# Where the end of a sliding-window attention stage puts its low parts, its last value banks and its first logits

## The reference, cut to what matters

```python
q, k, v, z = split(x @ w_in, [1024, 1152, 1280])        # 16 query heads, 2 key heads of 64; z is 1024 wide
q, k = rope(q), rope(k)
s = einsum(q_block, k_block_and_previous) * 64 ** -0.5   # window 128, blocks of 128 tokens
s = where(0 <= i + 128 - j < 128, s, -inf)
p = softmax(concat([s, sink]))[..., :-1]
o = einsum(p, v)
y = (o * silu(z)) @ w_out                                # 1024 x 1024
x = layernorm(4 ** 0.25 * x + y) * g + b
```

## Time and profile before

| what | before |
|---|---|
| three executions | 1002.01 to 1003.83 us, median 1003.71 |
| the profiled execution | 1004.43 us, of which its span 1002.7 us |
| busy of the span | PE 97%, DVE 64%, ACT 45%, POOL 34% |
| mean granted TensorE clock | 0.993 |
| matmuls, busy in 900 to 920 us | 12.01 of 20 us, clock 0.83 |
| matmuls, busy in 920 to 980 us | 60.00 of 60 us, clock 1.00 |

### The profile page before, as it was taken

The page is one execution under the profiler, slowest core; times in us unless marked ns, Lnnn a source line. Parts: engine busy times, 40 slices in busy tenths (PEclk is TensorE's granted clock), DMA queues, the critical chain, the costliest instruction groups (busy, mean ns, idle before and its releaser), DMA issues.

```text
span 1002.7 us, 19936 instructions
## 1 busy us (share of the span) xinstructions
PE 967.8 (97%) x7678; PEld 797.3 (80%) x7678; DVE 646.7 (64%) x1197; ACT 450.5 (45%) x1301; POOL 337.4 (34%) x642
## 2 busy tenths in 40 slices
PE   7999999999999999999999999999999999996997
PEld 6888788787878787888888888888787777775885
DVE  4677858686766777664457656653435678778755
ACT  5656456565667565655356211321214555564000
POOL 1008484846565555646100000100012353546000
PEclk9999999999999999999999999999999999998999
DMA  6233412314142314141303412320305010123111
GB/s 215 65 82 92 104 60 63 102 39 126 33 111 54 110 36 130 30 114 42 96 22 100 153 42 64 85 53 1 95 22 106 24 44 24 49 75 113 63 42 63
DMA packets 95181, 73.80 MB, mean 74 GB/s; under 512 B 32848, under 2 KB 84208, under 8 KB 95088
## 3 DMA queue, kind: packets, MB, share of 16 engines
q1 hardware_dynamic: 60768, 55.69, 19.1%
q10 hardware_dynamic: 34320, 16.84, 6.6%
HBM read 61.47 MB, written 11.04 MB: 72 GB/s over the span
## 4 chain that ended last, share of the span: by engine, by line
PE 81%; DVE 8%; ACT 6%; DMA 3%; issue 2%; ACTq 0%; DVEq 0%
PE ps L805 28%; PE ps L992 15%; PE ps L1165 9%; PE ps L1064 9%; PE ps L1005 2%; PE ps L1187 2%; PE ps L1149 2%; DVE tok L1577 2%; PE ps L962 1%; DMA ws_raw<-in_b_w_in 1%; PE ps L973 1%; PE ps L971 1%; PE ps L882 1%; PE ps L950 1%; PE ps L949 1%
## 5 line engine op out<-in xcount | busy, mean ns | idle before, releaser
L805 PE MATMUL ps<-act_hi,w_hi 128*128 128x512 f32 x512 | 224.2, 438 | 0.4 <-DVE w_lo L1528 0.4
L805 PE MATMUL ps<-act_hi,w_lo 128*128 128x512 f32 x512 | 201.6, 394 | 0.0
L805 PE MATMUL ps<-act_lo,w_hi 128*128 128x512 f32 x512 | 200.5, 392 | 0.0
L707 POOL TENSOR_TENSOR rank<-inverse,tok 128x60 f32<-128x60 f32 (+24 forms) x248 | 95.5, 385 | 97.9 <-DMA tok<-blocks_in 79.6
L1577 DVE SCALAR_TENSOR_TENSOR tok<-xs,convw,tok 128x512 f32<-128x512 f32 x144 | 116.3, 808 | 15.7 <-ACT xs L1290 13.7
L805 PEld LDWEIGHTS ps<-act_hi,w_lo 128*128 128x128 f32 x512 | 96.4, 188 | 21.4
L710 POOL TENSOR_TENSOR inverse<-inverse,rank 128x60 f32<-128x60 f32 (+24 forms) x248 | 102.0, 411 | 19.4
L805 PEld LDWEIGHTS ps<-act_hi,w_hi 128*128 128x128 f32 x512 | 97.3, 190 | 12.4 <-issue 0.6
L805 PEld LDWEIGHTS ps<-act_lo,w_hi 128*128 128x128 f32 x512 | 97.5, 190 | 10.0
L992 PE MATMUL ps<-wo_hi,act_hi 128*128 128x512 f32 x224 | 89.1, 398 | 8.9 <-DVE act_lo L1669 7.0
L992 PE MATMUL ps<-wo_lo,act_hi 128*128 128x512 f32 x224 | 88.2, 394 | 1.0 <-ACT bT L1490 1.0
(11 more groups left out here) (265 smaller groups left out, 2115.0 us busy)
## 6 DMA issues: line engine op xcount, KB each, us to landing
w_raw<-in_a_w_in ACTq DMA_DIRECT2D x32, 512.0 KB, 4.2
tok<-in_x SPq DMA_DIRECT2D x8, 512.0 KB, 7.4
decay<-gc_rows SPq DMA_DIRECT2D x8, 512.0 KB, 5.4
tok<-blocks_in SPq DMA_DIRECT2D x32, 128.0 KB, 2.7
v_turn<-v_tok SPq DMA_DIRECT2D x8, 512.0 KB, 6.4
v_tok<-v_turn SPq DMA_DIRECT2D x32, 128.0 KB, 3.0
xres<-in_x SPq DMA_DIRECT2D x8, 512.0 KB, 3.6
ws_raw<-in_b_w_in SPq DMA_DIRECT2D x16, 256.0 KB, 2.7
```

The source lines that it names most:

```text
L707: inner.next(pool.tensor_tensor(part, inverse[:, 0:rows, m:m + 1].broadcast_to([P, rows, w]), blocks[:, m:m + 1, m + 1:32].broadcast_to([P ...
L805: mm = pe.matmul(ps[:, g % 2, :], lhs[:, k, :], rhs[:, k, HALF * b:HALF * (b + 1)], start=(i == 0), stop=(i == GROUP - 1))
```

## The change

It has five parts.

1. `low_wo` of slices 1 to 7 goes from GpSimd to VectorE, among `low_out` and `apply_gate`: slices 1 and 2 by hand, slices 3 to 7 in `out_stage`, with one of the last three `apply_gate` behind each of slices 3, 4 and 5. The low part of slice 0 moves ahead of the last logits' second unit. `w_out` is fetched through two buffers and no longer three.
2. After `out_pair(1, 2)` TensorE makes slices 0, 1 and 2 of token tile 2; from slice 3 on it makes three token tiles per slice, and tiles 3 to 7 follow one by one.
3. `last_rows_bank` of pair 14 is bank 4, and that of pair 15 stays so; the first `out_step` no longer waits for `s_e` and `s_ob3`. For this the sides of all units are swapped (`unit`, `place`), and `values(14)` waits for all exponentials.
4. `logits(0)` is made after the projection of token tile 20, three projections ahead of the last. The mask of unit 0 and its maximum come ahead of the last rope on VectorE, its exponentials ahead of the last transpose's copy on ScalarE, where a small Exp after tile 20 precedes them. `TURN_BANKS` uses bank 5 in place of 3 from tile 16 on.
5. The 7 low parts of the gate weights go from GpSimd to VectorE, behind the first `inverted` of each even pair.

The core of the diff (in the new code `logits`, `exponentials` and `biased` only stand earlier in the file):

```diff
-TURN_BANKS = [2 + n % 2 for n in range(3 * NT - 3)] + [5, 5, 6]
+TURN_BANKS = [(2, 3 if n < 2 * NT else 5)[n % 2] for n in range(3 * NT - 3)] + [5, 5, 6]
+EARLY_LOGITS = 20
-EARLY, EARLY_OUT = (3, 2), (3, 3)
-OUT_SLOT = ((0, 1, 2, 0, 1, 0, 1, 3), (0, 1, 2, 0, 1, 2, 0, 1))
+EARLY, EARLY_OUT = (3, 3), (3, 3)
+OUT_SLOT = ((0, 1, 2, 0, 1, 0, 1, 3), (0, 1, 0, 1, 0, 1, 0, 1))
 def unit(v):
-    return k, (k + v) % 2, k // NT, k % NT
+    return k, (k + v + 1) % 2, k // NT, k % NT
 def last_rows_bank(k):
-    return 4 if k == PAIRS - 1 else 1 + 2 * ((k + 1) % 2)
+    return 4 if k >= PAIRS - 2 else 1 + 2 * (k % 2)
...
@@ gpsimd, the loop over units
-                if v % 4 == 0 and v // 4 + 1 < NK:
-                    low_gate(v // 4 + 1)
-            for k in range(1, NK):
...
-                pool.tensor_tensor(wo[1][1][k][:, :], out_raw[1][OUT_SLOT[1][k]], wo[1][0][k][:, :].bitcast(F32),
-                                   ALU.subtract).then_inc(L[1]["wolo"], 1)
@@ tensor, out_stage
                 for k in range(2 * i, NK):
                     out_pair(i, k)
-                for t in range(2, NT):
+                    if i == 1:
+                        if k == 2:
+                            pe.wait_ge(s_ob, PAIRS)
+                            pe.wait_ge(s_ob3, PAIRS)
+                            out_step(1, 2, 0)
+                            out_step(1, 2, 1)
+                        out_step(1, 2, k)
+                for t in range(2 + i, NT):
@@ tensor, projections
+                if n == EARLY_LOGITS:
+                    pe.wait_ge(q_c, 17)
+                    pe.wait_ge(q_tev, 2 * NT)
+                    logits(0)
@@ tensor, values
-                pe.wait_ge(s_e, min(2 * k + 3, UNITS))
+                pe.wait_ge(s_e, 2 * k + 3 if k < PAIRS - 2 else UNITS)
...
             pe.wait_ge(z_t, PAIRS)
-            pe.wait_ge(s_e, UNITS)
-            pe.wait_ge(s_ob3, PAIRS - 1)
             out_step(1, 0, 0)
             out_step(1, 1, 0)
+            pe.wait_ge(s_ob3, PAIRS - 1)
             values(PAIRS - 1)
@@ scalar, projections
+                if n == EARLY_LOGITS:
+                    act.wait_ge(q_c, 17)
+                    act.activation(corner[:, 0, 0:1], corner[:, 0, 0:1], ACT.Exp)
+                if n == 3 * NT - 1:
+                    act.wait_ge(q_rope, 3 * NT)
+                    exponentials(0)
@@ scalar, end
             high_wo(1, 1)
             high_out(1, 1)
+            high_wo(1, 2)
+            high_out(1, 2)
             last_rows(PAIRS - 1)
-            high_out(1, 2)
             out_stage(1)
@@ vector, out_stage
                 for k in range(NK):
+                    if i == 1 and k >= EARLY[i]:
+                        low_wo(i, k)
                     if k >= EARLY_OUT[i]:
                         low_out(i, k)
...
+                    if i == 1 and k >= EARLY[i] and APPLIED[13 - EARLY[i] + k:]:
+                        apply_gate(APPLIED[13 - EARLY[i] + k])
@@ vector, projections
+                if n == 3 * NT - 1:
+                    dve.wait_ge(q_c, 17)
+                    biased(0)
@@ vector, in biased
+                if v == 0:
+                    dve.wait_ge(q_group, 3 * NT)
                 dve.tensor_reduce(sm["neg"][:, k % 2, x, :], keys[:, :, 0:WIDE + 1], mybir.AxisListType.X, ALU.max,
                                   negate=True).then_inc(s_neg, 1)
@@ vector, pairs
-            for k in range(PAIRS - 1):
+            for k in range(PAIRS - 2):
...
                 inverted(2 * k + 2)
+                if k % 2 == 0 and k // 2 + 1 < NK:
+                    low_gate(k // 2 + 1)
                 for g in APPLY_AT.get(k, ()):
                     apply_gate(g)
                 inverted(2 * k + 3)
                 gate(k + 1)
+            apply_gate(14)
+            biased(UNITS - 2)
+            low_wo(1, 0)
+            biased(UNITS - 1)
+            turned(UNITS - 4)
+            inverted(UNITS - 2)
+            turned(UNITS - 3)
+            branch(PAIRS - 3)
+            inverted(UNITS - 1)
+            low_out(1, 0)
+            gate(PAIRS - 1)
             turned(UNITS - 2)
             branch(PAIRS - 2)
             turned(UNITS - 1)
+            low_wo(1, 1)
             low_out(1, 1)
             branch(PAIRS - 1)
+            low_wo(1, 2)
             low_out(1, 2)
-            for g in APPLIED[-4:]:
-                apply_gate(g)
+            apply_gate(9)
             out_stage(1)
```

149 lines of the change are left out of this document (72 added, 77 removed).

## The result

The changed kernel took 991.32 us (median of four executions, 990.08 to 991.49), the kernel before 1003.25 beside it. The ratio is 0.988, its 95% interval 0.9863 to 0.9897. The forecast was 992.3. The profiled execution took 991.26 us (its span is 989.4), 13.2 us less than the profiled execution of before, which at 1004.43 lay 1.2 us above the median of 1003.25.

The account below looks back on a forecast made before the run. TensorE, busy 97% of the span, bounds the kernel, so only its idle pieces could be won. End 10.9 + head 1.3 - loop 0.5 = 11.7 us: 992.7 profiled, 992.0 against the median; forecast 992.3, range 990.7 to 996.2.

Parts of the forecast that it names:

- The end: End of attention, output projection of layer 1: 11.7 us of idle and half clock, less 0.8 remaining, gives 10.9.
- its idle term: Idle remaining at the end: 0.4 us at the first `out_step`, 0.2 at slice 1, 0.2 at slice 2.
- The forecast of no cost for three tiles: Output projection: VectorE clears tile 0's banks in 2.0 us, TensorE has 2.8 of other tiles; cost 0.
- The head: First logits of layer 1: TensorE's 1.4 us wait for pair 0's exponentials goes; gain 1.3, bounds 0.6 and 1.4.
- one sign: Pair loop: a TensorE wait for `zg` of 0.3 to 0.4 in pair 8, none in pairs 0, 2 and 10.
- The chain of exponentials: First logits: last rope ends at 763.2, ScalarE's exponentials of pair 0 at 766.9, 0.5 us ahead of TensorE.
- The step on the table load: First logits: the 1.28 us load ahead of the exponentials is made after tile 20, some 20 us earlier.
- The loop: Pair loop, gates' low parts on VectorE: pair 8 0.35 us behind TensorE; cost 0.5 taken, bounds 0 and 8.4.
- VectorE's chain did not starve TensorE: Rival, end of attention: seven more low parts on VectorE starve TensorE, 3.5 us, giving 996; chance 0.14.
- The loop did not become VectorE's: Rival, pair loop: low parts cost in most even pairs, 4 to 8 us, giving 996 to 1000; chance 0.07.
- No slice from 3 on came late: Rival, output projection: slice 3 still late by 4 us or more, clock falls again, giving 998; chance 0.05.
- The slower case: Rival, pair loop: VectorE bounds every pair, lock waits of 4.7 us per double pair, 1005 to 1008; chance 0.04.

Follow-up runs that it names:

- by writing: Changed kernel with fourteen GpSimd memsets of 128x1024 added from about 896 us, which only write SBUF; 991.15 us in one run.
- part 2 alone: Kernel before with only token tile 2 made beside tiles 0 and 1, three tiles a slice; 998.99 us, ratio 0.9955.
- order alone: Kernel before with the last three `apply_gate` one behind each of slices 3 to 5, low parts still on GpSimd; 999.61 us, ratio 0.9965.
- GpSimd reading: Changed kernel with six more GpSimd `tensor_tensor` reading two SBUF tiles, from 894.8 us on; 997.42 us in one run.
- part 1 undone: Changed kernel with low parts of slices 1 to 7 back on GpSimd, `apply_gate` still one by one; 991.75 us, ratio 0.9896.
- part 1 alone: Kernel before with low parts of slices 1 to 7 on VectorE and the last four `apply_gate` one by one; 994.87 us, ratio 0.9925.
- part 2 undone: Changed kernel with two token tiles a slice, token tile 2 back among those that follow; 993.79 us, ratio 0.9909.
- the version without it: Changed kernel with both reciprocals of a pair behind its low part and `apply_gate`, without pair 8's stall; 991.03 us, ratio 0.9865.

## Why the prediction was right, and where its sizes were off

*The end: forecast 10.9, measured 12.1.* The mechanism was right: the `apply_gate` were drawn out by GpSimd's reading of SBUF beside them (GpSimd made busy by reading brings 7.4 back, by writing nothing), and the half clock stood behind the long wait and went with it. Two terms of the sum were too small. First, the idle that remains was forecast as 0.4 + 0.2 + 0.2 and is 0.20 in the records, at slice 1, as forecast; the other two places show no wait. At the first `out_step` the gate was forecast to end 7.3 us behind the start of gate group 15 and ended 7.1 behind it. TensorE started 0.14 behind that, about 0.2 later than it could have (the values and what follows them lie 1.57 apart there and 1.36 in the loop), which is too short for a recorded wait. Second, a stop costs more than its recorded wait, which the sum left out: its idle term held waits alone. The wait counts from the record's end of the last matmul, and a matmul lasts 0.39 in the record while the next would start 0.23 after it: 0.16. The first matmul behind a stop holds the next back for 0.31 in place of 0.23: 0.08. With 0.24 for each stop more than the changed kernel's one, the ends come out like this:

| kernel | end | more than changed | waits more | clock | stops | sum |
|---|---|---|---|---|---|---|
| before | 108.85 | 12.09 | 9.68 | 1.77 | 3: 0.72 | 12.17 |
| part 2 alone | 104.44 | 7.68 | 5.59 | 1.47 | 3: 0.72 | 7.78 |
| order alone | 105.44 | 8.68 | 6.86 | 0 | 7: 1.68 | 8.54 |
| GpSimd reading | 104.19 | 7.43 | 5.25 | 1.34 | 3: 0.72 | 7.31 |
| part 1 undone | 98.48 | 1.72 | 1.47 | 0 | 1: 0.24 | 1.71 |
| part 1 alone | 100.42 | 3.66 | 2.40 | 0 | 2: 0.48 | 2.88 |
| part 2 undone | 98.79 | 2.03 | 1.28 | 0 | 1: 0.24 | 1.52 |

(The clock is the time that the matmuls behind the long wait took, less 0.23 each; in these rows 0.08 of one stop is in both columns.) Five rows come out within 0.2, so the 0.24 is an estimate from record lengths that the ends bear out. The last two rows miss 0.8 and 0.5. Both have two tiles a slice and VectorE at 2.87 against TensorE's 2.8, which gives hesitations under the record's limit; by the starts of the matmuls they are 0.6 in all in part 1 alone and 0.3 in part 2 undone. The rest I can't place.

*Which part did it.* The prediction priced the end as a whole. The runs take it apart by three switches: the order (`apply_gate` one by one), the engine of the low parts, and the cover (three tiles).

| order | engine | cover | end | run |
|---|---|---|---|---|
| block | GpSimd | two | 108.85 | before |
| one by one | GpSimd | two | 105.44 | order alone |
| block | GpSimd | three | 104.44 | part 2 alone |
| one by one | VectorE | two | 100.42 | part 1 alone |
| one by one | VectorE | two | 98.79 | part 2 undone |
| one by one | GpSimd | three | 98.48 | part 1 undone |
| one by one | VectorE | three | 96.76 | changed |

From the kernel before, the order gives 3.4 and the engine 5.0 more. With order and cover in place the engine is worth only 1.7, and with order and engine in place the cover 2.0: these two stand in for each other. The last three rows have everything else of the change besides, the four above them don't; 100.42 against 98.79 shows what that rest makes of the end, 1.6. In it are part 3, which costs 0.3 when undone, and ScalarE's new list, which no run has alone. The forecast of no cost for three tiles held: the residual of tile 0 waits for TensorE, and no wait of TensorE follows.

*The head: forecast 1.3, measured 1.20.* The wait of 1.39 went and the gate became the next late thing, at 0.26, just over the forecast's 0 to 0.2; so one sign failed, that no wait for `zg` would show in pair 0. The chain of exponentials was forecast 0.5 ahead of TensorE and was 1.2 ahead, since the last rope began 0.65 later than before and not 1.4. The step on the table load was wrong without harm: it moved 16 us ahead, not 20, and was not what made the difference.

*The loop: forecast +0.5, measured +0.14.* The stall of pair 8 came as worked out (0.35 on TensorE, forecast 0.35) and for the reason given, the normalisation in front of the two `apply_gate`; by the version without it, it is worth 0.40. The 0.5 was this and a margin for which the prediction gives no row. What was missed is a gain elsewhere: the block of logits that is 0.26 longer wherever the gates' low parts are on GpSimd. 0.40 - 0.26 = 0.14, as measured; the cause of the 0.26 stays open.

*The time.* The sum for the profiled execution was 992.7 and it took 991.26. The three errors, -1.2 at the end, +0.1 at the head and -0.4 in the loop, make -1.5. The medians lie 11.9 apart, nearer to the forecast's 11.7 than the pieces' 13.15 are; that nearness is luck, since the start of layer 1 alone moves by 2 us.

*The rivals.* VectorE's chain did not starve TensorE, since each of its instructions ran at its lone duration. The loop did not become VectorE's: one pair of 16 stalls. No slice from 3 on came late in the changed kernel; slice 6 did, by 1.29, with two tiles a slice. The slower case needed lock waits of 4.7 us in each double pair; pair 8 has 1.2.

## What to carry to other kernels

When two engines' waits trace back to instructions that last three or four times their usual, look what runs beside them before you reorder: reordering the queue gave 3.4 us at the end, and moving the low parts off GpSimd 5.0 more. Give the engine that must not wait some work that hangs on nothing ahead of the stretch where others are late: with an extra tile a slice even the slow instructions cost only 1.7. Price each part twice, added to the old kernel and taken from the new one, for the two prices differ. And count stops as well as waited time, since one long wait that becomes seven short ones keeps seven restarts.

## What the runs showed of the hardware

- A VectorE `tensor_tensor` with both inputs in SBUF beside GpSimd instructions that read SBUF takes 2.8 to 3.4 us when both engines go without a gap, at 512 as at 1024 columns, where alone it takes 0.68 and 1.22; where they overlap in part, 1.4 to 2.6 were seen (part 1 undone). GpSimd pays too: its subtract of 128x1024 takes 2.40 with little beside it and 3.23 on the mean of six. Beside GpSimd memsets (1.01 each) nothing changes.
- TensorE's clock fell to half behind waits of 6.97, 3.57 and 2.90 us and stayed at 2.4 GHz behind waits of 1.32 and less. What the half clock cost did not follow the wait: 1.77, 1.34 and 1.47 us. So shortening the long wait from 7.0 to 2.9 gave back only 0.3 of the clock's cost.
- A stop of TensorE between matmuls of 128x512 costs some 0.24 us beyond the wait in its record, an estimate from record lengths (0.16 + 0.08) that five of seven ends bear out within 0.2.
- A table load of 1.28 us in a gap that ScalarE had anyway cost nothing.
